# Softmax division moved from the probabilities to the attention outputs, with divisor rows made by TensorE

## What is computed

```python
# dense (context queries, and the grouped heads)
p = jax.nn.softmax(s, axis=-1)
o = einsum('bkgqs,bskd->bqkgd', p, v)
# neighbourhood (latent queries: local keys and all context keys in one softmax)
p = jax.nn.softmax(jnp.concatenate([s_loc, s_ctx], axis=-1), axis=-1)
o = einsum(p[..., :n_loc], vb) + einsum(p[..., n_loc:], ctx_v)
out = concatenate([oa, ob]) @ w_out
```

## Time and profile before

| | |
|---|---|
| median of 3 runs | 1561.33 us (1559.12 to 1562.13) |
| profiled execution, its own time | 1559.92 us |
| span of its instructions | 1558.1 us |
| TensorE busy | 98% (9159 matmul instructions) |
| VectorE busy | 69% |
| ScalarE busy | 40% |
| granted TensorE clock, mean | 0.995 of full speed |

### The profile page before, as it was taken

One profiled execution on the slowest core, in us unless ns is written; L12 is line 12 of the kernel. 1 busy time (PEld: TensorE's weight loads), 2 busy tenths in 40 slices (PEclk: granted clock), 3 DMA queues, 4 the chain that ended last, 5 costly groups with the idle time before them and its releaser, 6 DMA issues.

```text
span 1558.1 us, 23355 instructions
## 1 busy us (share of the span) xinstructions
PE 1519.7 (98%) x9159; PEld 1491.8 (96%) x9159; DVE 1073.2 (69%) x1423; ACT 616.3 (40%) x840; POOL 74.0 (5%) x59
## 2 busy tenths in 40 slices
PE   6999999989899999999999999999999999999999
PEld 6899999989759999999999999999999999999999
DVE  6886777868897866768877667797767567443323
ACT  3452332164583643322355233226643246333221
POOL 2000000023100100000020000002000010000000
PEclk9999999989999999999999999999999999999999
DMA  9345465736403244465624545563552533333332
GB/s 386 112 141 211 166 228 205 261 139 230 139 1 140 104 172 178 180 250 193 241 86 154 220 162 216 216 252 130 195 206 82 216 109 108 135 111 133 135 112 91
DMA packets 49937, 262.68 MB, mean 169 GB/s; under 512 B 6608, under 2 KB 7888, under 8 KB 27984
## 3 DMA queue, kind: packets, MB, share of 16 engines
q1 hardware_dynamic: 49872, 261.79, 45.9%
HBM read 259.54 MB, written 2.23 MB: 168 GB/s over the span
## 4 chain that ended last, share of the span: by engine, by line
PE 84%; DVE 6%; issue 4%; DMA 2%; ACT 2%; SPq 1%; POOL 0%; DVEq 0%; ACTq 0%
PE ps L1288 24%; PE ps L1290 24%; PE ps L1289 24%; PE ps L1322 3%; PE ps L1325 3%; PE ps L1323 3%; DVE mprod L827 2%; ACT w_hi L537 1%; DMA raw<-panels 1%; DMA raw_x<-panels 1%; DVE x_lo L890 1%; DVE w_lo L819 1%; DVE h L1011 1%; PE ps L1612 1%; PE ps L1516 1%
## 5 line engine op out<-in xcount | busy, mean ns | idle before, releaser
L819 DVE TENSOR_TENSOR w_lo<-raw,w_hi 128x2048 fp32r<-128x2048 f32 x163 | 373.2, 2289 | 305.0 <-ACT w_hi L537 303.6
L537 ACT ACTIVATE w_hi<-raw 128x2048 fp32r<-128x2048 f32 x164 | 314.2, 1916 | 666.7 <-PE ps L1290 506.4
L1288 PE MATMUL ps<-x_hi,w_hi 128*128 128x384 f32 (+1 forms) x1520 | 515.9, 339 | 9.8 <-DVE x_lo L890 8.6
L1289 PE MATMUL ps<-x_lo,w_hi 128*128 128x384 f32 (+1 forms) x1520 | 513.1, 338 | 0.0
L1290 PE MATMUL ps<-x_hi,w_lo 128*128 128x384 f32 (+1 forms) x1520 | 512.7, 337 | 0.0
L827 DVE SCALAR_TENSOR_TENSOR mprod<-mraw,cB 128x1024 f32<-128x1024 f32 x256 | 313.2, 1224 | 7.8
L1288 PEld LDWEIGHTS ps<-x_hi,w_hi 128*128 128x128 f32 x1520 | 286.6, 189 | 13.2 <-issue 7.4
L1289 PEld LDWEIGHTS ps<-x_lo,w_hi 128*128 128x128 f32 x1520 | 286.9, 189 | 0.7
L1290 PEld LDWEIGHTS ps<-x_hi,w_lo 128*128 128x128 f32 x1520 | 286.6, 189 | 0.0
L1290 PE MATMUL ps<-act_hi,w_lo 128*128 (+1 forms) x832 | 279.6, 336 | 0.0
L1288 PE MATMUL ps<-act_hi,w_hi 128*128 (+1 forms) x832 | 279.6, 336 | 0.0
(11 more groups left out here) (154 smaller groups left out, 1148.4 us busy)
## 6 DMA issues: line engine op xcount, KB each, us to landing
raw<-panels SPq DMA_DIRECT2D x164, 1024.0 KB, 5.2
mraw<-mod_rows SPq DMA_DIRECT2D x128, 512.0 KB, 3.5
raw_x<-panels SPq DMA_DIRECT2D x5, 1024.0 KB, 6.0
mshift<-mod_rows SPq DMA_DIRECT2D x8, 512.0 KB, 15.5
mscale<-mod_scale SPq DMA_DIRECT2D x6, 512.0 KB, 12.2
bias<-na_bias SPq DMA_DIRECT2D x4, 512.0 KB, 6.4
h<-x_in_t SPq DMA_DIRECT2D x1, 1536.0 KB, 11.0
out<-h SPq DMA_DIRECT2D x4, 384.0 KB, 2.3
```

What stands on the lines that cost most here:

```text
L537: nc.scalar.activation(w_hi[q0 % 2][:, :], raw[q0 % 2][:, :], ACT.Copy).then_inc(hi_done, 1)
L819: nc.vector.tensor_tensor(w_lo[q0 % 2][:, :], raw[q0 % 2][:, :], w_hi[q0 % 2][:, :].bitcast(F32), ALU.subtract).then_inc(lo_done, 1)
L1288: mm(out, w[0][:, cols], xs[0], start=start, stop=False)
L1289: mm(out, w[0][:, cols], xs[1], start=False, stop=False)
```

## The change

The probabilities are transposed and multiplied with the values without being normalised. Once a turn, VectorE writes the reciprocals of the turn's six sums per query, each repeated 64 times, as a 128x384 tile (`divisor`); TensorE transposes it in three blocks into PSUM bank 2 (`divisor_rows`), which gives a tile with the divisor of every output element; ScalarE copies it to SBUF (`put_divisor`); VectorE multiplies the output in PSUM bank 7 with it into `tmp` (`o_divided`); `o_hi` and `o_lo` then read `tmp`. The outputs have one bank where they had two. `p_transposes` waits for the exponentials alone. The sums are kept in two sets, by turn.

```diff
+                if s >= 6 and s % 3 == 0:
+                    act.wait_ge(rinv_done, s // 3 - 1)
...
+            def put_divisor(turn):
+                act.wait_ge(div_pe, turn + 1)
+                if turn:
+                    act.wait_ge(o_scaled, turn)
+                nc.scalar.activation(tmp[:, 1, 0:T], ps[:, DIV_BANK, 0:T], ACT.Copy).then_inc(div_done, 1)
+
             def o_hi(turn):
-                act.wait_ge(o_pe, turn + 1)
-                nc.scalar.activation(x_hi[:, TURNS[turn], 0:T], ps[:, O_BANK[turn % 2], 0:T], ACT.Copy).then_inc(oh_done, 1)
+                act.wait_ge(o_scaled, turn + 1)
+                nc.scalar.activation(x_hi[:, TURNS[turn], 0:T], tmp[:, 0, 0:T], ACT.Copy).then_inc(oh_done, 1)
...
             for i in range(STEPS):
                 put_pT(i)
+                if i and i % 3 == 0:
+                    put_divisor(i // 3 - 1)
                 if i + 2 < STEPS:
                     softmax(i + 2)
...
-                if i and i % 3 == 0:
+                if i > 3 and i % 3 == 1:
                     o_hi(i // 3 - 1)
+            put_divisor(7)
             o_hi(7)
...
-            def normalise(s):
-                dve.wait_ge(exp_done, s + 1)
-                link(nc.vector.reciprocal(rinv[:, s % 3, :], rsum[:, s % 3, :]))
-                v = prob[:, s % 3, :, 0:span(s)]
-                nc.vector.tensor_tensor(v, v, rinv[:, s % 3, :, None].to_broadcast([P, 2, span(s)]), ALU.mult) \
-                    .then_inc(prob_done, 1)
+            def divisor(turn):
+                dve.wait_ge(exp_done, 3 * turn + 3)
+                if turn:
+                    dve.wait_ge(div_pe, turn)
+                nc.vector.reciprocal(tmp[:, 2, 0:T].rearrange("p (t a d) -> p t a d", a=2, d=HD),
+                                     rsum[:, turn % 2, :, :, None].to_broadcast([P, TT, 2, HD])).then_inc(rinv_done, 1)
+
+            def o_divided(turn):
+                dve.wait_ge(o_pe, turn + 1)
+                if turn:
+                    dve.wait_ge(ol_done, turn)
+                dve.wait_ge(div_done, turn + 1)
+                nc.vector.tensor_tensor(tmp[:, 0, 0:T], ps[:, O_BANK, 0:T], tmp[:, 1, 0:T], ALU.mult) \
+                    .then_inc(o_scaled, 1)
...
-            normalise(0)
             for i in range(STEPS):
                 if i + 2 < STEPS:
                     top(i + 2)
-                if i + 1 < STEPS:
-                    normalise(i + 1)
-                if i > 3 and i % 3 == 1:
-                    o_lo(i // 3 - 1)
+                if i and i % 3 == 0:
+                    o_divided(i // 3 - 1)
+                if i % 3 == 2:
+                    divisor(i // 3)
+                    if i > 3:
+                        o_lo(i // 3 - 1)
+            o_divided(7)
             o_lo(7)
...
             def p_transposes(s):
-                pe.wait_ge(prob_done, s + 1)
+                pe.wait_ge(exp_done, s + 1)
...
+            def divisor_rows(turn):
+                pe.wait_ge(rinv_done, turn + 1)
+                if turn:
+                    pe.wait_ge(div_done, turn)
+                for t in range(TT):
+                    last = nc.tensor.transpose(ps[:, DIV_BANK, P * t:P * t + P], tmp[:, 2, P * t:P * t + P], ident[:, :])
+                last.then_inc(div_pe, 1)
+
             def values(turn):
 
                 pair = TURNS[turn]
+                if turn:
+                    pe.wait_ge(o_scaled, turn)
                 pe.wait_ge(pT_done, 3 * turn + 3)
-                if turn >= 2:
-                    pe.wait_ge(ol_done, turn - 1)
...
                     scores(i + 2)
+                if i == 3:
+                    pe.wait_ge(tr_act, 13)
+                if i and i % 3 == 0:
+                    divisor_rows(i // 3 - 1)
                 p_transposes(i)
...
                 some((5, 6))
                 p_transposes(STEPS - 1)
                 some((0, 1))
+                divisor_rows(NH - 1)
                 values(NH - 1)
                 return some((4, 3, 7, 2))
```

More of the change, by code:

```diff
@@ L141, in build @@
         nmax = sb("nmax", [P, 3, 2])
-        rsum = sb("rsum", [P, 3, 2])
-        rinv = sb("rinv", [P, 3, 2])
+        rsum = sb("rsum", [P, 2, 3, 2])
         vss = sb("vss", [P, TT, KD])
@@ L262, in build @@
         exp_done = sem("exp_done")
-        prob_done = sem("prob_done")
+        rinv_done = sem("rinv_done")
+        o_scaled = sem("o_scaled")
+        div_pe = sem("div_pe")
+        div_done = sem("div_done")
         pT_pe = sem("pT_pe")
@@ L692, in _ @@
                 if g == 7:
-                    nc.scalar.activation(rsum[:, 2, 0:1], mhalf[:, 0:1], ACT.Exp)
+                    nc.scalar.activation(rsum[:, 0, 2, 0:1], mhalf[:, 0:1], ACT.Exp)
                 for i in TR_AFTER[g]:
@@ L701, in softmax @@
                     act.wait_ge(pT_pe, s - 2)
+                if s >= 6 and s % 3 == 0:
+                    act.wait_ge(rinv_done, s // 3 - 1)
                 for a in range(2):
                     last = nc.scalar.activation(prob[:, s % 3, a, 0:span(s)], scored(s)[:, a, :], ACT.Exp,
-                                                bias=nmax[:, s % 3, a:a + 1], accum_out=rsum[:, s % 3, a:a + 1])
+                                                bias=nmax[:, s % 3, a:a + 1], accum_out=rsum[:, s // 3 % 2, s % 3, a:a + 1])
                 last.then_inc(exp_done, 1)
@@ L1170, in top @@
                 nc.vector.tensor_reduce(nmax[:, s % 3, :], scored(s), AX.X, ALU.max, negate=True).then_inc(nmax_done, 1)
-            def normalise(s):
-                dve.wait_ge(exp_done, s + 1)
-                link(nc.vector.reciprocal(rinv[:, s % 3, :], rsum[:, s % 3, :]))
-                v = prob[:, s % 3, :, 0:span(s)]
-                nc.vector.tensor_tensor(v, v, rinv[:, s % 3, :, None].to_broadcast([P, 2, span(s)]), ALU.mult) \
-                    .then_inc(prob_done, 1)
+            def divisor(turn):
[11 more added lines that the diff above has]
+                    .then_inc(o_scaled, 1)
             def o_lo(turn):
-                pair = TURNS[turn]
+                dve.wait_ge(o_scaled, turn + 1)
                 dve.wait_ge(oh_done, turn + 1)
-                nc.vector.tensor_tensor(x_lo[:, pair, 0:T], ps[:, O_BANK[turn % 2], 0:T], x_hi[:, pair, 0:T].bitcast(F32),
+                nc.vector.tensor_tensor(x_lo[:, TURNS[turn], 0:T], tmp[:, 0, 0:T], x_hi[:, TURNS[turn], 0:T].bitcast(F32),
                                         ALU.subtract).then_inc(ol_done, 1)
@@ L1531, in values @@
                         moving = pT_ctx[:, turn % 2, a, :] if keys < 0 else pT_lat[:, a, keys, :]
-                        last = mm(ps[HD * a:HD * a + HD, O_BANK[turn % 2], out_cols], w, moving, start=start, stop=stop)
+                        last = mm(ps[HD * a:HD * a + HD, O_BANK, out_cols], w, moving, start=start, stop=stop)
                 last.then_inc(o_pe, 1)
@@ L1554, in _ @@
                     transposed(j)
-                if i == 3:
-                    pe.wait_ge(tr_act, 13)
                 if i and i % 3 == 0:
@@ L1562, in ready_attn @@
                     pe.wait_ge(exp_done, STEPS - 1)
+                    pe.wait_ge(ol_done, 6)
                 elif m == 0:
@@ L1567, in ready_attn @@
                 elif m == 7:
-                    pe.wait_ge(ol_done, 7)
+                    pe.wait_ge(o_scaled, 8)
                 elif m == 2:
@@ L1652 @@
 S_BANK = (5, 0)
-O_BANK = (7, 2)
+O_BANK, DIV_BANK = 7, 2
 TR_AFTER = ((), (), (), (), (0, 1), (2, 3), (4, 5), (6, 7), ())
@@ L1663, in tr_bank @@
 def tr_bank(i):
-    return 3 + i % 2 if i < 8 else O_BANK[i % 2]
+    return 3 + i % 2 if i < 8 else (O_BANK, DIV_BANK)[i % 2]
 _OUTS = [(P, KD, T), (1, 1, NCTX, NH, HD), (1, 1, NCTX, NH, HD), (1, 1, NCTX, 2, HD), (1, 1, NCTX, 2, HD)]
```

## The result

The changed kernel takes 1578.74 us in the median of 4 runs (1575.93 to 1580.86), the kernel before 1560.22 (1558.16 to 1562.13). The ratio is 1.0118, 95% interval 1.0096 to 1.014: slower, about 18 us, where I had forecast 1560.6 and a range of 1557 to 1567. The profiled execution took 1579.33 us, with a span of 1577.5.

A forecast was written before the change was run, and what follows sets the result against it. TensorE's own queue was taken to bound attention, with two-turn periods of 13.08 us against 13.05. Terms -1.5 (first steps), +0.1 (middle), +0.7 (last steps) gave -0.7 us: 1560.6 from the median 1561.33, range 1557 to 1567.

The forecast's parts named there:

- 128x384 is not in the trace ... I take 0.55: VectorE's new divisor reciprocal, once a turn: length taken as 0.55 us from `o_lo`'s 384 elements, another operation.
- Equal medians, so nothing says that an element costs more: VectorE, 2-element instructions: reciprocal 155 ns and TENSOR_TENSOR 155 ns in the median, taken as no extra price per element.
- The bound from above: Upper bound for the 128x384 reciprocal on VectorE: 7.5 ns an element from slowest against fastest, 3.0 us.
- slow reciprocal: Rival: VectorE's divisor reciprocal takes 3.0 us and TensorE waits for it; total about +14 us, 1575; chance 0.12.
- the whole sum: Whole kernel: first steps -1.5, three middle periods +0.1, last steps +0.7, together -0.7 us.
- the first steps: Start of attention: without normalisation waits, 2.21 us saved less 0.72 for transposes, so first values 1.49 us earlier.
- What bounds attention: Attention's two-turn period: TensorE's own work is 11.54 of 13.05 us; removable waits are 0.97 us.
- the bank loop: TensorE transposes and ScalarE copies sharing two single banks: 1.84 us loop, leaving 0.18 us waits twice a period after the change.
- the divisor transposes: Three added TensorE transposes a turn, 0.35 us each turn, 0.70 a period; 0.52 a turn as upper bound.
- The clock after: First steps: low clock from 420.20 to 423.30 taken as gone with the 1.54 us wait; otherwise 0.8 of the gain lost.
- The last steps: End of attention: -0.23 without normalisation, +0.35 for divisor transposes, +0.58 at the passage to the next panel; sum +0.70 us.
- Handover: From last values to the projection's next weight panel: `o_divided` goes ahead of `o_hi` and the split, +0.58 us uncovered.

The follow-up runs named there:

- e3: Kernel before plus VectorE reciprocals of 2 to 128 and 384 elements and a copy of 384, where VectorE waits for turn 7's values; one profiled execution 1565.14 us.
- e4: On top of e2, the short reciprocal and spreading copy queued on VectorE ahead of the next turn's maximum; 1560.75 us, ratio 0.9987 to the kernel before.
- c2: Kernel before, unedited, run again as a control for the clock; single execution 1564.00 us.
- e6: Kernel before with only the second weight panel's split moved ahead of the last turn's `o_hi` and `o_lo`; ratio 0.9988 to the kernel before.
- c5: Kernel before, unedited, run again as a control for the clock; single execution 1560.32 us.
- c1: Changed kernel, unedited, as a control; median of 4 1581.19 us, ratio 1.0126 to the kernel before.
- c3: Changed kernel, unedited, run again as a control for the clock; single execution 1579.45 us.
- c4: Changed kernel, unedited, run again as a control for the clock; single execution 1572.90 us.
- e1: Changed kernel with the 128x384 reciprocal replaced by a copy of the sums (wrong results, for time alone); ratio 1.0007 to the kernel before.
- e2: Changed kernel with the reciprocal taken of the six sums alone, then a copy spreading it over 128x384; ratio 1.0002 to the kernel before.
- e5: On top of e2 and e4, the second weight panel's split queued ahead of the last turn's output work; 1560.40 us, ratio 0.9984 to the kernel before.

## Why the prediction was wrong

**The step that failed** is "128x384 is not in the trace ... I take 0.55". It measured 2.54. I read the price of an element from an instruction of 2 elements, where 156 ns is a floor under which 6.25 ns an element show as little as 1.04 (e3). "Equal medians, so nothing says that an element costs more" was true and said nothing. The bound from above, 3.0 us from the extremes, held; the rows gave no reason for a weight as low as 0.12 near it.

The outcome is the rival "slow reciprocal", by its mechanism. Its own sum with 2.54 in place of 0.55 gives waits of 3.17 + 1.99 - 2.69 = 2.47 and 2.45 + 1.99 - 2.69 = 1.75; measured 2.48 and 1.74. Period 11.54 + 0.70 + 0.36 + 2.47 + 1.75 = 16.82; measured 16.77. The Trainium skill ("VectorE: DVE Perf Modes", "First, the fixed hardware budget") has the repeat count of 8; by an estimate, as eight steps of 1.04 ns, it would be 8.3 ns an element, and measured is 6.25. It pointed the right way where the trace was silent.

That the rival's 1575 stands near the measured 1578.7 is in part luck: it was worked out for 3.0 us. With 2.54 the whole sum gives about 1572 (1561.3 - 0.7 + 3 x 3.74), some 7 us short. Missing in it are the clock's share and the first steps, below.

**What bounds attention: right.** TensorE's own queue left 0.97 us a period to win, whatever VectorE gave up. With the divisor tile off the path (e4) a period is 12.54, 0.51 below 13.05: 11.54 own, 0.36 of the bank loop, and what is left, 0.64, for the divisor transposes, which I had at 0.70. VectorE is busy 9.30 us of that period in place of 11.90, and the 2.6 us bought half a microsecond.

**The bank loop** (0.18 us twice a period): right, and still there in the changed kernel without any normalisation to blame.

**The first steps: right against the trace they were worked out from, and nil against another of the same kernel.** I forecast the first values 1.49 us earlier. They come 12.73 after the first scores (418.30 to 431.03), against 14.29 in the first trace: 1.56. But that trace has the low clock there, and the kernel before without it needs 12.70 (c2; 12.68 in e6, whose edit comes later). At full clock group 12's copy comes 0.66 us earlier (12.04 after the first scores against 12.70), and the divisor and kind 0 transposes behind it take 0.69. So the -1.5 in the sum is the price of a low stretch, and not of the waits that I booked as saved. Of the five traces with the old first steps three have that stretch (before, c5, e3) and two have not (c2, e6).

**The clock after.** I took one low stretch as removed, with the 1.54 us wait ahead of it. None is in the first steps in any of the eight traces with the change (after, c1, c3, c4, e1, e2, e4, e5). But the wait alone doesn't decide it: c2 has it too, 1.53 us at 425.50, at full clock. And behind the changed kernel's 3.03 us stalls one or two low stretches, which cost 1.6 us each, came into the turns, in all four traces. The variants without those stalls (e1, e2, e4, e5) have none in attention: granted clock 1.00 from the first scores to the second panel.

**The last steps: right.** Values of turn 6 to values of turn 7: 7.69 against 7.59, +0.10 (forecast -0.23 + 0.35 = +0.12). Handover 7.09 against 6.45, +0.64 (forecast +0.58). Moving the split ahead removes it (e5), and even part of what the kernel before lost (e6).

**The sum, on traces with the same clock ahead of attention** (after and c2): three periods 53.5 against 39.2, +14.4, of which 11.2 are the reciprocal at full clock and 3.2 the two low stretches; +0.1 and +0.6 at the end. Together 15.1, and the split ends 80.98 against 65.85 after the first scores, 15.1. Spans: 1577.5 - 1562.2 = 15.3. The medians differ by 18.5, and by 19.9 in the control. Where do the 3 to 5 us between come from? The four traces of the changed kernel span 1571.1 to 1577.7, the three of the kernel before 1558.1 to 1562.2, and none shows a further loss. The record has the span and the mean granted clock of almost every execution, and span times clock is an estimate of what the span would be at full clock. Over 10 executions of the changed kernel (mean span 1577.0) it averages 1563.0, over 51 of the kernel before (mean span 1560.4) 1551.3. That is 11.7 us apart, and the traces give 11.9 at full clock (three times 3.72, and 0.7 at the end). The rest of the spans, the share lost to the clock, averages 14.0 us against 9.1. So of the 16.7 us between the mean spans the clock carries about 5, of which attention's low stretches are 3.2 at most. The clock is on record to 0.001, which is 1.6 us of a span, so only the averages say this much. Where the executions without a trace lose the rest is open.

## What to carry to other kernels

A price per element can't be read from an instruction of two elements; if the same operation on many is the heart of a change and the trace has none, give the high bound real weight. Do an expensive operation on the small tile and spread the result with a copy: 0.18 + 0.55 us in place of 2.54. Before taking a load off a busy engine, subtract the own times of the engine it feeds from the period: that difference is all there is to win.

## What I had not expected of the hardware

- RECIPROCAL on VectorE, float32, 128 partitions: 156 ns for 2 elements, 203 for 16, and from 32 on 98 + 6.25 n ns (898 for 128, 2496 for 384; 2542 with each of 6 values repeated 64 times); a copy of 384 took 497 (e3).
- A copy on VectorE of 6 sums spread over 384 elements took 351 ns from `rsum` (e1) and 553 from `vss`, a source with a longer stride (e2). Why they differ wasn't tried.
- The same instructions ahead of attention began attention at 412.4 to 418.1 us in three traces of one kernel, through stretches of the lower granted clock (0.53 over 54.80 to 61.70 in one, 1.00 over the same window in the first). Single traces are compared only after looking at these.
- After a wait of the same length the granted clock fell in one place and not in another: 7 of 12 stalls of 3.03 us in the changed kernel, and the wait of 1.54 us in the first steps of the kernel before in 3 of 5 traces.
